# Turning half of the gathered expert rows on VectorE instead of TensorE, in a decoder step with 64 experts

## What is computed

```python
def step(acc, blk):
    e, tok, wt = blk
    xb = h[tok]                                   # gathered rows, 128 to a block
    hb = jax.nn.silu(xb @ we_g[e]) * (xb @ we_u[e])
    return acc.at[tok].add(wt[:, None] * (hb @ we_d[e]).astype(jnp.float32)), None
```

## Time and profile before

| what | value |
|---|---|
| median of the runs | 1125.21 us |
| the profiled execution | 1126.64 us |
| its span, first to last instruction | 1124.8 us |
| TensorE busy | 1094.1 us, 97% of the span |
| VectorE busy | 462.7 us, 41% |
| ScalarE busy | 236.4 us, 21% |
| GpSimd busy | 135.3 us, 12% |
| moved by DMA | 337.16 MB, mean 300 GB/s |

### The profile page before, as it was taken

How to read it: one execution, slowest core, us unless ns; L and a number is a source line. 1 busy time by engine, 2 the same in 40 slices (tenths; PEclk the granted TensorE clock), 3 DMA queues, 4 the chain that set the end, 5 groups by cost and what they waited for, 6 DMA issues and landing times.

```text
span 1124.8 us, 16922 instructions
## 1 busy us (share of the span) xinstructions
PE 1094.1 (97%) x6443; PEld 575.1 (51%) x6443; DVE 462.7 (41%) x1286; ACT 236.4 (21%) x516; POOL 135.3 (12%) x163
## 2 busy tenths in 40 slices
PE   6999999999999999999999999999999999999896
PEld 3456677777877545754343443443444444343232
DVE  2218541565456645843274233233232232331157
ACT  4131241222133123211111111111111111111111
POOL 0210000000020010121112112111111121121100
PEclk9999999999999999999999999999999999999999
DMA  9857622021170273899999999999999999999598
GB/s 370 326 207 295 227 79 75 1 85 51 62 266 7 103 255 120 311 365 426 423 425 426 424 417 425 425 416 396 421 409 384 426 399 400 417 391 370 209 412 344
DMA packets 51655, 337.16 MB, mean 300 GB/s; under 512 B 9637, under 2 KB 14089, under 8 KB 30831
## 3 DMA queue, kind: packets, MB, share of 16 engines
q1 hardware_dynamic: 33710, 287.32, 63.0%
q0 software_dynamic: 17856, 48.68, 11.8%
HBM read 311.30 MB, written 37.24 MB: 310 GB/s over the span
## 4 chain that ended last, share of the span: by engine, by line
PE 91%; DMA 4%; DVE 2%; ACT 1%; issue 1%; SPq 0%; DVEq 0%; POOLq 0%; ACTq 0%
PE bank L1561 30%; PE bank L1584 15%; PE bank L1257 10%; PE bank L1276 5%; PE bank L1549 4%; DMA mem<-expert_out_rows 3%; PE bank L1375 3%; PE bank L1376 3%; PE bank L1170 3%; PE bank L1493 3%; PE bank L1254 3%; PE bank L1145 1%; PE bank L1572 1%; PE bank L1340 1%; PE bank L1154 1%; PE bank L1128 1%
## 5 line engine op out<-in xcount | busy, mean ns | idle before, releaser
L1561 PE MATMUL bank<-mem 128*32 128x512 f32 (+2 forms) x1488 | 304.5, 594 | 0.6 <-DVE mem L2247 0.6
L1561 PEld LDWEIGHTS bank<-mem 128*32 128x32 f32 (+2 forms) x1488 | 100.6, 126 | 166.0 <-issue 166.0
L1584 PE MATMUL bank<-mem 128*32 128x512 f32 (+2 forms) x744 | 157.0, 596 | 0.1
L2247 DVE COPY mem<-bank 128x512 f32<-128x512 f32 x48 | 33.2, 691 | 283.3 <-PE bank L1549 283.3
L1257 PE MATMUL bank<-hT,mem 128*128 128x288 f32 x512 | 133.3, 410 | 1.0 <-ACT mem L935 1.0
L1257 PEld LDWEIGHTS bank<-hT,mem 128*128 128x128 f32 x512 | 93.9, 190 | 25.7 <-issue 2.4
L1561 PE MATMUL bank<-x_sb,mem 128*32 128x512 f32 (+2 forms) x416 | 99.3, 594 | 0.0
L1065 ACT ACTIVATE mem<-bank 128x256 f32<-128x256 f32 x48 | 18.4, 384 | 313.0 <-PE bank L1572 312.8
L1584 PEld LDWEIGHTS bank<-mem 128*32 128x32 f32 (+2 forms) x744 | 48.7, 126 | 61.4 <-issue 60.6
L2262 DVE COPY hT<-bank 128x512 f32<-128x512 f32 x48 | 33.2, 691 | 85.7 <-PE bank L1584 85.6
L790 POOL DMA_INDIRECT mem<-ffn_in_rows,idxg x32 | 32.9, 1028 | 264.5 <-DVE idxs L2243 211.0
(11 more groups left out here) (400 smaller groups left out, 1281.2 us busy)
## 6 DMA issues: line engine op xcount, KB each, us to landing
mem<-k_w_exp SPq DMA_DIRECT2D x51, 2048.0 KB, 23.3
mem<-in_w_exp_down SPq DMA_DIRECT2D x51, 1024.0 KB, 22.7
x_sb<-k_w_exp SPq DMA_DIRECT2D x13, 2048.0 KB, 21.4
mem<-k_w_ada SPq DMA_DIRECT2D x8, 2048.0 KB, 9.0
mem<-k_w_in SPq DMA_DIRECT2D x7, 2048.0 KB, 9.7
hT<-in_w_exp_down SPq DMA_DIRECT2D x13, 1024.0 KB, 25.4
mem<-expert_out_rows SPq DMA_DIRECT2D x6, 2048.0 KB, 16.5
mem<-k_w_head SPq DMA_DIRECT2D x4, 2048.0 KB, 18.4
```

The costliest lines, as they stand in the source:

```text
L1561: i = mm(bank[sl, :], xT[:, j % 2, c * BLK + sl.start:c * BLK + sl.stop], wview(r)[0][:, c, :], start=c == 0, stop=c == KC - 1)
L1584: i = mm(ps[4 + hf][sl, :], hhT[:, k * BLK + sl.start:k * BLK + sl.stop], wview(r)[1][:, k, hf * 512:(hf + 1) * 512], start=k == 0, stop=k ...
```

## The change

TensorE turns four chunks instead of eight, into bank 0 alone. VectorE's copy of bank 1 goes. In its place `turn` writes the other four chunks of `xT` straight from the gathered rows, by 16 instructions of VectorE's own 32x32 transpose: each takes 32 partitions and, in the four chunks, 32 columns each, 128 elements per partition, and turns the four pieces. It waits for the gather itself and, since it overwrites a half of `xT` that an earlier block's `up` has read, for `eup`. Who wants to reuse a gather buffer now waits for both turns (`xgT_t` and `xgT_d`).

```diff
@@ gpsimd, ahead(n, q, g) @@
                 elif n >= XG:
                     pool.wait_ge(S["xgT_t"], n - XG + 1)
+                    pool.wait_ge(S["xgT_d"], n - XG + 1)
@@ tensor, x_T(n, j, s) @@
                 if not (isinstance(n, int) and n == 0):
                     pe.wait_ge(S["xgT_a"], n)
-                    pe.wait_ge(S["xgT_d"], n)
                 else:
                     pe.wait_ge(S["sh_ready"], NSH - 1)
-                for c in range(KC):
-                    i = tr(ps[c // 4][:, (c % 4) * BLK:(c % 4 + 1) * BLK], xg[g][:, c * P:(c + 1) * P], ident[:, :])
+                for c in range(KC // 2):
+                    i = tr(ps[0][:, c * BLK:(c + 1) * BLK], xg[g][:, c * P:(c + 1) * P], ident[:, :])
                 i.then_inc(S["xgT_t"], 1)
@@ vector @@
-            def xT_evac(n, j):
-                dve.wait_ge(S["xgT_t"], n + 1)
-                cp(xT[:, j % 2, 4 * BLK:8 * BLK], ps[1][:, :]).then_inc(S["xgT_d"], 1)
+            def turn(n, j, s=None):
+
+                g = gbuf(n, j)
+                dve.wait_ge(S[f"gat{g}"], gcount(n, j, s))
+                if not (isinstance(n, int) and n < 2):
+                    dve.wait_ge(S["eup"], n - 1)
+                rows = xg[g][:, 4 * P:8 * P].rearrange("s (c d) -> s c d", c=KC // 2)
+                cols = xT[:, j % 2, 4 * BLK:8 * BLK].rearrange("d (c s) -> d c s", c=KC // 2)
+                for q in range(P // QS):
+                    for a in range(P // QS):
+                        sl, dl = slice(q * QS, (q + 1) * QS), slice(a * QS, (a + 1) * QS)
+                        i = dve.transpose(cols[dl, :, sl], rows[sl, :, dl])
+                i.then_inc(S["xgT_d"], 1)
@@ vector, the loop over blocks @@
                 if b < NBK - 1:
-                    xT_evac(b + 1, b + 1)
+                    turn(b + 1, b + 1)
                 gated(b, b)
```

More of the change, by code:

```diff
@@ L646, in _ @@
             sp.wait_ge(S["xgT_t"], NBK)
+            sp.wait_ge(S["xgT_d"], NBK)
             for t in range(NT):
@@ L796, in ahead @@
                     pool.wait_ge(S["xgT_t"], n - 1)
+                    pool.wait_ge(S["xgT_d"], n - 1)
                 elif n >= XG:
                     pool.wait_ge(S["xgT_t"], n - XG + 1)
+                    pool.wait_ge(S["xgT_d"], n - XG + 1)
                 pool.sem_inc(S["pool_step"], 1)
@@ L2266, in body @@
                 gated(n, j)
-                xT_evac(n + 1, j + 1)
+                turn(n + 1, j + 1, s + 1)
                 idx_out(n + 2, j + 2, s + 2)
@@ L2280, in _ @@
             place(2)
-            xT_evac(0, 0)
+            turn(0, 0)
             shared_mul(NSH - 1)
@@ L2302, in first_blocks @@
                 place_more(NBK + 1, NBK + 1, 1)
-                xT_evac(NBK, NBK)
+                turn(NBK, 0, 0)
                 idx_out(NBK + 1, NBK + 1)
```

## The result

| | before | changed |
|---|---|---|
| median of the runs | 1125.40 us (1124.67 to 1125.9, 4 runs) | 1132.28 us (1131.54 to 1133.8, 4 runs) |
| ratio | | 1.0063, 95% interval 1.0046 to 1.0081 |
| the profiled execution | 1126.64 us | 1131.54 us |
| its span | 1124.8 us | 1129.7 us |
| TensorE busy | 1094.1 us | 1083.9 us |

The changed kernel is slower by 0.6%, some 7 us. The forecast was 9.6 us faster, and its range ended at 1124. The prediction was wrong in sign and in range.

A forecast was written before the change was run, and what follows sets the result against it. TensorE and the DMA engines were both taken as full. 20 x 0.41 - 2.2 = 6.0 us of lead, cut to 0.7 at block 21, less 1.7 for clock, grew to 9.6 by block 47: 1115.6 us, range 1108 to 1124.

The forecast's parts named there:

- TensorE's part: In each block, four of eight turns go from TensorE: 0.41 us saved a block (0.33 to 0.435).
- VectorE's part: In each block, 16 transposes of 0.265 us, 4.2 us in all (3.0 to 5.5), replace a copy of 691 ns.
- So: nothing on the path: In each block, VectorE's work queued behind the transposes delays nothing on the path: transposes end before `gated` could start.
- The start: At the start of the expert stage nothing covers the transposes: `up` starts 2.2 us later (1.0 to 3.5).
- The load lands at 734.7 as before: At block 21, the expert load's landing stays at 734.7, cutting TensorE's lead from 6.0 to 0.7 us.
- 0.02 x 141 = 2.8 us of idle DMA time can be used: Between 735 and 876 us, loads issued earlier can use 2.8 us of idle DMA time, so block 33 doesn't wait.
- no wait: At blocks 25 and 33, TensorE's leads of 0.6 and 3.9 us cause no wait for expert loads.
- a lead of 9.6 us: At block 47, TensorE is 9.6 us ahead of the old schedule, and the work after it starts that much earlier.
- The cost of the wait: After block 21's wait, a lower clock costs another 1.7 us of work, leaving the lead at -1.0.
- (b): Rival for the expert stage: the DMA engines set the pace to the end, gain some 1.5 us, 1123.7; chance 0.18.
- (c): Rival: VectorE becomes the bound from 0.55 us a transpose; at 0.7 us the kernel takes 1214; chance 0.06.

The follow-up runs named there:

- e11: Changed kernel, blocks 0, 1 and 7 to 10 turned the old way, half the down weights unloaded from the sixth expert on: 1110.12 us (kernel before, so lightened: 1125.93).
- e7: Changed kernel with half the down weights not loaded from the sixth expert on: 1117.41 us (kernel before with the same lighter loads: 1125.93).
- e8: Changed kernel with blocks 7 to 10, which share VectorE with the table, turned the old way: 1129.50 us, 1.0038 of the kernel before.
- e5: Kernel before with VectorE's 16 transposes added in blocks 11 to 47, ahead of its copy, which overwrites them: 1129.62 us, ratio 1.0035.
- e9: Kernel before with 16 one-element copies per partition added on VectorE in blocks 11 to 47: 1128.47 us, ratio 1.0021.
- e1: Kernel before with only four of eight chunks turned on TensorE, the other four left unturned, no transposes added: 1125.17 us, ratio 0.9997.
- e3: Changed kernel with blocks 0, 1 and 7 to 10 turned the old way, all weights loaded: 1128.49 us, 1.0026 of the kernel before.
- e10: Kernel before with seven 128x512 multiplications added on VectorE in blocks 11 to 47: 1126.57 us, ratio 1.0004.
- e4: Changed kernel with only blocks 0 and 1 turned the old way: 1131.16 us, 1.0050 of the kernel before.

## Why the prediction was wrong

- **TensorE's part: right.** The turns of a block take 0.44 us less. In e11 42 of the 48 blocks are turned the new way for 15.8 us, 0.38 us each; the step had 0.41.
- **VectorE's part: the size off a little, the cover overlooked.** The step took 0.265 us a transpose; it is 0.302, and 0.315 from start to start (5.04/16). The Trainium skill's 58 + FD cycles ("VectorE: DVE Perf Modes", The TRN2 errata), which gave 194 ns, doesn't hold here. The same section adds that the fixed part was measured at about 150 cycles; as an estimate by that, (150 + 128)/0.96 = 290 ns, which is near the trace. The rule of the Trainium skill's same page (Rules for kernel authors) to give a 128x128 turn to TensorE where a PSUM destination will do came out right here with all weights loaded; with lighter loads the turn on VectorE won 8.5 and 15.8 us (e7, e11).
- **"So: nothing on the path": the first step that failed.** I checked what is queued behind the transposes in a common block and not in every block. `table` adds 7.2 us in block 7, which with 5.0 us of transposes and the rest of VectorE's work is more than a block of 11.6 us holds. Cost: 3.6 us in the trace, 2.8 us by e8, where the step had nothing.
- **The start: half right.** The step had 2.2 us (1.0 to 3.5); it is 2.9. That TensorE's idle time there would also cost clock, as I had counted for block 21, was left out: 1.5 us more.
- **"The load lands at 734.7 as before": the second step that failed.** It lands at 739.2. One microsecond is the later issue (707.7 against 706.7). The other 3.5 us are a longer way, 31.5 against 28.0 us, of which e5 shows 3.0 with no other change in the kernel. I had no term for a landing that moves, by VectorE's instructions (e5, e9) or otherwise: counted from the first turn it comes 0.9 us later even in e1, which adds nothing. The cause stays open.
- **"0.02 x 141 = 2.8 us of idle DMA time can be used": the third step that failed, and the one by which the gain went to nothing.** The share of 0.99 is no reserve. In e1, where nothing is in the way, block 47 starts only 1.4 to 2.9 us earlier, and the medians are level. The step also looked at three gate-and-up loads alone, while e1 waits 4.6 us for down loads, the first time near 566 us. The changed kernel waits at block 33 and at block 46, where I had predicted "no wait". Of a lead of 9.6 us hardly anything could have been kept, so any disturbance had to show as a loss.
- **The cost of the wait: right for this wait, partly by luck.** After 4.16 us of idle time the product takes 8.48 us in place of 7.00, 1.5 us more; the step had 1.7. Elsewhere the cost is anything from nothing to 2.9 us, as the last section says. In the trace of the changed kernel the stretch right after the wait, with the clock third from the end:

```profile
739.40:742.80 3.40, 3.40 (x20) 0.97 (x24) 2.41 (x8) 0.00 (x0) 0.00 (x0) 0.58 1.04 437
```

The granted clock is 0.58: most of it is at the lower level, 1.2 GHz in place of 2.4, although TensorE works all through it.

Of the rivals, (b), the DMA engines set the pace to the end, was the true one for what TensorE saves: it forecast 1.5 us of gain, and e1 shows 0.3 us by its ratio and 1.4 to 2.9 in its trace. I gave it 0.18. It took its 1.5 us from the slack of three loads, so that it comes this near is in part luck. (c), VectorE becomes the bound, was wrong as a whole, with 0.302 us against its threshold of 0.55, but true in one block of 48 and at the start. No rival had the losses on top. The sum, as the runs give it: TensorE's saving about 0 (e1), start and table together 0.37% or 4.2 us (e3 against the change), and the remaining 0.26% or 2.9 us, of the same size as e9's 0.21% and e5's 0.35%. That it is the same effect is argued from this size and from the wait at block 21 (3.2 us in e3); how more instructions on VectorE delay a load stays open. No version that I ran beats the kernel before with all its weights loaded.

## What to carry to other kernels

When two resources are full at once, relieving one is worth the slack of the other: read it from the last load that is waited for (landing against use), not from a mean share: here shares of 0.98 to 1.01 left no room, and 0.91 did. A work-around that adds instructions to an engine has to be followed through every block, the odd one included, and a schedule with 0.7 us of slack in one load can lose several times that from work which looks covered. Test it by halves: the saving alone, the cost alone, and both with the other limit taken away.

## What the hardware showed that I had not expected

- With sixteen more short instructions a block on VectorE, and nothing else changed, a load landed 3 us later and the kernel was 0.2 to 0.35% slower (e5, e9). With seven long ones and the same busy time as e5 it landed some 1.5 us later, which the slack took up, and the time was the same (e10).
- A wait for a load often costs more than its length, through the clock: 8.4 to 8.8 us for the next product in place of 7.0 or 7.1, after waits of 2.36 us (e9), 2.38 (e5), 2.73 (e1) and 4.16, 2.48 and 2.76 us (the changed kernel), and 9.95 us after 3.22 us (e3, block 21), where the granted clock was 0.50 from 738 to 742 us. It is not sure to: after 0.90 us (e10), 1.82 us (e1, block 46), 2.53 us (e3, block 17) and even 3.69 us (e4, block 21) the product took 7.1 us, in e4 at a granted clock of 1.00 throughout. After 2.39 us ahead of e1's last block it took 5.37 us, as in the changed kernel after no wait to speak of. What tells the two kinds of wait apart, no run shows, but it is not the length alone.
